# Token halves in the down projections, and linear attention's norm taken with tokens on partitions

## The reference

```python
h = layer_norm(concat([meta, x]))
h = layer_norm(alpha * h + 0.5 * swiglu(h, gate1, up1, down1))
h = layer_norm(alpha * h + token_mixer(h, w_in, ...) )
h = layer_norm(alpha * h + 0.5 * swiglu(h, gate2, up2, down2))
return h[:, N_META:]

def swiglu(h, w_gate, w_up, w_down):
    return (silu(h @ w_gate) * (h @ w_up)) @ w_down

# in token_mixer, behind one input projection: window attention (8 heads, 2 key heads, blocks of 128)
# beside gated linear attention (4 heads, both directions, chunks); its end, per head of 128 values:
    o = o * lax.rsqrt(jnp.mean(o * o, axis=-1, keepdims=True) + LN_EPS) * norm_g
    return o.reshape(b, t, GLA_WIDTH) * jax.nn.silu(g)
```

## Time and profile before

| | us |
|---|---|
| median of 3 runs | 1091.71 |
| the runs | 1092.06, 1083.59, 1091.71 |
| the profiled execution | 1082.67 |
| its span, first to last instruction | 1080.9 |
| busy: TensorE, VectorE, ScalarE | 997.0, 720.4, 382.2 |
| first down projection, from 283.5 to 396.2 | 112.7 |
| LN1 and first projections, to 428.6 | 32.4 |
| LN2, from 682.0 to 717.4 | 35.4 |
| second down projection, from 951.8 to 1059.6 | 107.8 |
| LN3 and the stores | 21.3 |

### The profile page before, as it was taken

The page is one execution under the profiler, slowest core; times in us unless marked ns, Lnnn a source line. Parts: engine busy times, 40 slices in busy tenths (PEclk is TensorE's granted clock), DMA queues, the critical chain, the costliest instruction groups (busy, mean ns, idle before and its releaser), DMA issues.

```text
span 1080.9 us, 16392 instructions
## 1 busy us (share of the span) xinstructions
PE 997.0 (92%) x6605; PEld 654.4 (61%) x6605; DVE 720.4 (67%) x1186; ACT 382.2 (35%) x488; POOL 32.3 (3%) x96
## 2 busy tenths in 40 slices
PE   3999999999899988999996889699999999989995
PEld 2888888888688875985564434434444444434443
DVE  6766666668755667767659757666666667966645
ACT  5422222224411126754334741462222223531105
POOL 0000000000000000000000000000000000000000
PEclk9999999999899998999998999889999999999998
DMA  5323232323232121111211003112323223322202
GB/s 203 107 79 109 85 110 84 109 86 110 105 108 85 68 78 32 62 64 42 77 40 40 1 1 117 40 73 83 116 78 116 96 98 127 111 78 86 104 1 79
DMA packets 23808, 88.76 MB, mean 82 GB/s; under 512 B 2907, under 2 KB 3251, under 8 KB 23763
## 3 DMA queue, kind: packets, MB, share of 16 engines
q1 hardware_dynamic: 22752, 87.17, 22.7%
q10 hardware_dynamic: 1011, 0.99, 0.3%
HBM read 86.05 MB, written 2.10 MB: 82 GB/s over the span
## 4 chain that ended last, share of the span: by engine, by line
PE 75%; DVE 16%; ACT 6%; issue 2%; DMA 0%; ACTq 0%; POOL 0%; DVEq 0%
PE PS L553 35%; PE PS L593 20%; PE PS L648 8%; DVE cmax L1413 3%; DVE wsp L1435 3%; PE PS L944 3%; ACT wsp L1059 2%; PE PS L510 2%; PE PS L632 1%; DVE big L1513 1%; ACT H L1053 1%; PE PS L770 1%; DVE X L1363 1%; PE PS L922 1%; PE PS L766 1%
## 5 line engine op out<-in xcount | busy, mean ns | idle before, releaser
L553 PE MATMUL PS<-xs,wsp 128*128 128x264 f16 (+1 forms) x3168 | 472.7, 312 | 7.5 <-ACT xs L1051 4.0
L553 PEld LDWEIGHTS PS<-xs,wsp 128*128 128x128 f16 x3168 | 311.0, 98 | 168.4 <-issue 9.6
L1059 ACT ACTIVATE wsp<-stage,wscale 128x2048 f16<-128x2048 f32 (+2 forms) x73 | 156.5, 2144 | 369.9 <-DVE wscale L1399 198.0
L1435 DVE SCALAR_TENSOR_TENSOR wsp<-stage,wscale,wsp 128x2048 f16<-128x2048 f32 (+2 forms) x73 | 184.6, 2529 | 114.3 <-ACT wsp L1059 114.3
L593 PE MATMUL PS<-big,wsp 128*128 128x264 f16 (+1 forms) x1584 | 238.6, 314 | 11.6 <-DVE big L1513 9.5
L593 PEld LDWEIGHTS PS<-big,wsp 128*128 128x128 f16 x1584 | 155.8, 99 | 94.1 <-DVE big L1513 12.8
L1413 DVE TENSOR_REDUCE cmax<-stage 128x1 f32<-128x2048 f32 (+2 forms) x73 | 179.7, 2462 | 3.9
L1447 DVE SCALAR_TENSOR_TENSOR big<-PS,oscale,tmp_a 128x528 f32 (+3 forms) x44 | 33.4, 759 | 75.7 <-ACT tmp_a L1066 75.6
L1066 ACT ACTIVATE tmp_a<-PS,oscale 128x528 f32<-128x528 f32 (+1 forms) x44 | 30.5, 694 | 136.1 <-PE PS L553 136.1
L648 PE MATMUL PS<-xs,wsp 128*128 128x264 f16 (+1 forms) x384 | 67.0, 328 | 0.1
L2007 POOL PARTITION_ALL_REDUCE call<-cmax x73 | 27.9, 382 | 979.1 <-DVE cmax L1413 979.1
(11 more groups left out here) (208 smaller groups left out, 685.1 us busy)
## 6 DMA issues: line engine op xcount, KB each, us to landing
stage<-in_gate SPq DMA_DIRECT2D x44, 512.0 KB, 3.4
stage<-in_up SPq DMA_DIRECT2D x44, 512.0 KB, 4.2
stage<-in_down SPq DMA_DIRECT2D x32, 704.0 KB, 4.9
stage<-in_w_in SPq DMA_DIRECT2D x16, 512.0 KB, 4.4
stage<-in_w_out SPq DMA_DIRECT2D x8, 512.0 KB, 4.4
X<-in_x SPq DMA_DIRECT2D x4, 512.0 KB, 6.2
out_T<-H SPq DMA_DIRECT2D x8, 256.0 KB, 2.0
stage<-in_w_in SPq DMA_DIRECT2D x2, 576.0 KB, 4.4
```

The lines of the kernel that those rows point to most:

```text
L553: return nc.tensor.matmul(dst, w, x, start=k == 0 and wp + xp == 0, stop=k == KD - 1 and xp == 1)
L1059: nc.scalar.activation(wsp[:, slot, 0, 0:cols], stage[:, slot, 0:cols], ACT.Copy, scale=wscale[:, slot:slot + 1]).then_inc(w_hi, 1)
L1435: nc.vector.scalar_tensor_tensor(wsp[:, slot, 1, 0:cols], stage[:, slot, 0:cols], wscale[:, one], wsp[:, slot, 0, 0:cols], ALU.mult, ALU.s ...
```

## The change

In both down projections tiles 0 to 4 stay whole; tiles 5, 6 and 7 are computed for the first half of the tokens, then for the second. Their weights stay in a third place (`w_extra`, in the arena), and chunks are loaded and prepared in the order 0, 1, 5, 2, 3, 6, 4, 7. The norm of half 0 runs on the other engines while TensorE multiplies half 1; half 0's mean and squares are put between the tiles of half 1. After the first down projection the first projections are taken by halves too, with other banks, and `gates(1)` comes behind both gq tiles. LN1's second half is done under them. The output leaves in 16 stores of half a tile. In LN2 VectorE takes the low half of the next chunk ahead of the last residual, the maximum behind the centring, the scale behind the reciprocals. ScalarE calls Sqrt once at the head of each norm. In the linear attention's norm the squares are the stationary operand of products with one column of `ones_dv`, so that the mean lands with tokens on partitions, 4 columns for a head; Sqrt and reciprocal run on those, the result scales an identity, and a product with `ones_dv` spreads it over the partitions into PSUM, where the last product reads it.

The diff, cut to its core:

```diff
+N_FULL = 5
+DN_ORDER = [0, 1, 5, 2, 3, 6, 4, 7]
 @@ SyncE
+                for n, q in enumerate(DN_ORDER):
+                    sp.wait_ge(w_ready, DN[f] + n - 1)
+                    load_halves(down[f][q], (DN[f] + n) % 2, DN_COLS)
 @@ TensorE, down projection
+                for q in range(N_FULL):
+                    down_tile(f, q)
+                down_tile(f, 5, 0)
+                down_tile(f, 6, 0)
+                down_tile(f, 7, 0, (KF - 3, lambda: sum_tiles(L, 0)))
+                down_tile(f, 5, 1, (8, lambda: mean(L, 0)))
+                square_sums(L, 0)
+                down_tile(f, 6, 1)
+                down_tile(f, 7, 1, (KF - 3, lambda: sum_tiles(L, 1)))
 @@ TensorE, mixer (first_proj_tiles(0) has mean(1, 1) at its third step)
+                first_proj_tiles(0)
+                square_sums(1, 1)
+                early_proj_tile(GK + 1, 0)
+                early_proj_tile(GQ, 0)
+                first_proj_tiles(1)
+                early_proj_tile(GK + 1, 1)
                 gates(0)
+                early_proj_tile(GQ, 1)
+                proj_tile(GQ + 1)
                 gates(1)
 @@ TensorE, norm
                 gla_step(1, 5)
+                norm_spread(0)
                 proj_half(AQ + 3, 1)
+                norm_spread(1)
                 proj_half(AK, 0)
                 norm_sums(2)
                 proj_half(AK, 1)
                 norm_sums(3)
                 proj_half(AV, 0)
+                norm_spread(2)
                 proj_half(AV, 1)
+                norm_spread(3)
 @@ ScalarE, mixer
+                proj_out(GQ)
                 gates_abs(0)
+                projection_hi(2)
+                proj_out(GQ + 1)
                 gates_abs(1)
-                projection_hi(2)
-                gates_ln(0)
-                proj_out(GQ)
-                proj_out(GQ + 1)
+                gates_ln(0, GV)
                 projection_hi(3)
-                proj_out(GV)
                 decays(0, 0)
                 proj_out(GV + 1)
 @@ VectorE, down projection (next_* act on the chunk that is n-th in DN_ORDER)
+                next_max(2)
+                next_scale(2)
+                next_max(3)
+                next_lo(2)
+                next_scale(3)
+                down_residual(f, 0)
+                next_lo(3)
+                next_max(4)
+                next_scale(4)
+                next_max(5)
+                next_scale(5)
+                down_residual(f, 1)
+                next_lo(4)
+                next_lo(5)
+                next_max(6)
+                next_scale(6)
+                down_residual(f, 2)
+                next_max(7)
+                next_lo(6)
+                next_scale(7)
+                next_lo(7)
+                down_residual(f, 3)
...
+                down_residual(f, 7, 0)
+                centre(L, 0)
+                down_residual(f, 5, 1)
+                half_rstd(L, 0)
+                half_norm(L, 0, 0, 4)
+                down_residual(f, 6, 1)
+                half_norm(L, 0, 4, KD)
+                down_residual(f, 7, 1)
+                centre(L, 1)
+                half_rstd(L, 1)
+                half_norm(L, 1, 0, KD)
 @@ VectorE, mixer and norm
                 projection_max(3)
+                projection_scale(3)
                 gates(0)
-                projection_scale(3)
                 gates(1)
...
+            def norm_diag(h):
+                nc.vector.reciprocal(o_root[:, h, :], o_root[:, h, :]).then_inc(o_rstd, 1)
...
+                nc.vector.tensor_tensor(o_diags[j][:, a, N_META:T].rearrange("p (b t) -> p b t", b=NB),
+                                        ident[:, :].unsqueeze(1).to_broadcast([P, NB, P]),
+                                        o_root[:, h, :].unsqueeze(2).to_broadcast([P, NB, P]), ALU.mult).then_inc(o_diag, 1)
 @@ VectorE, output projection and LN2
                 for t in range(2):
-                    residual_tile(2 * n + t, t, KD + 2 * n + t, c % 2, 2)
-
-            chunk_lo(GU[1], GU[1] % 2, GU_COLS)
-            chunk_max(GU[1] + 1, (GU[1] + 1) % 2, (GU[1] + 1) // 2, GU_COLS)
+                    if last and t:
+                        chunk_lo(c + 1, (c + 1) % 2, cols)
+                    residual_tile(2 * n + t, t, c % 2)
```

More of the change, by code:

```diff
@@ L493, in _, with sum_tiles @@
+            sp.wait_ge(out_done, 2 * 16 * KD)
         @block.tensor
         def _(pe):
-            def sum_tiles(L):
-                pe.wait_ge(x_summed, sums_before(L) + N_SUM)
-                for h in range(2):
-                    nc.tensor.matmul(PS[:, ln_bank(L, 0, h), 0:ln_width(L)], ones[:, :], x_sum[:, token_half(L, h)], start=True, stop=False)
+            def sum_tiles(L, h):
+                pe.wait_ge(x_summed, sums_before(L) + (N_SUM if L == 2 or h == 0 else KD))
+                nc.tensor.matmul(PS[:, ln_bank(L, 0, h), 0:ln_width(L)], ones[:, :], x_sum[:, token_half(L, h)], start=True, stop=False)
@@ new lines, in mean, with square_sums @@
+            def mean(L, h):
+                if L == 2:
+                    pe.wait_ge(*((res_half, 1) if h == 0 else (res_done, 2 + RES[3])))
+                else:
+                    pe.wait_ge(res_done, 2 + RES[L] + N_DN + (N_DN - N_FULL) * h)
+                nc.tensor.matmul(PS[:, ln_bank(L, 0, h), 0:ln_width(L)], ones[:, :], X[:, KD - 1, token_half(L, h)],
+                                 start=False, stop=True).then_inc(mean_ready, 1)
+            def square_sums(L, h):
+                for k in range(KD):
+                    n = ln_step(L, h, k)
+                    pe.wait_ge(squared, n + 1)
+                    nc.tensor.matmul(PS[:, ln_bank(L, 1, h), 0:ln_width(L)], ones[:, :], squares[:, n % 4, 0:ln_width(L)],
+                                     start=k == 0, stop=k == KD - 1).then_inc(sq_added, 1)
@@ L572, in gu_tile, with down_tile @@
                 mm.then_inc(gu_ready, 1)
-            def res_tile(late, r, s, w, src, kt, k_sem=None, k0=0, norm=None, split_at=None, before_b=None):
+            def down_tile(f, q, h=None, between=None):
+                i = q if h != 1 else q + N_DN - N_FULL
+                s = i % 2
+                r = RES[2 * f + 1] + i
+                pe.wait_ge(w_ready, DN[f] + DN_AT[q] + 1)
                 pe.wait_ge(res_done, r + 1)
-                for k in range(kt):
-                    if norm is not None and k == kt - 3:
-                        sum_tiles(norm)
-                    if k == split_at:
+                for k in range(KF):
+                    if between is not None and k == between[0]:
+                        between[1]()
+                    if k == KF_A:
@@ L976, in _ @@
             ffn(1)
-            layer_norm(3)
+            mean(3, 1)
+            square_sums(3, 1)
         @block.scalar
@@ new lines, in ffn @@
+                for n in range(2):
+                    down_scales(n)
+                next_max(2)
[13 more added lines that the diff above has]
+                next_max(6)
```

403 lines of the change are left out of this document (249 added, 154 removed).

## The result

The changed kernel takes 1099.56 us (median of 18 runs, 1091.10 to 1106.57) against 1089.07 for the kernel before (18 runs beside it, 1082.64 to 1092.26): ratio 1.0102, 95% interval 1.0077 to 1.0126, so 11 us slower. The forecast was 1088.5, the range ended at 1098. The profiled execution of the changed kernel took 1097.0 us, with a span of 1095.2, against 1082.67 and 1080.9.

The account below looks back on a forecast made before the run. TensorE bounds both down projections, VectorE and ScalarE handing units to each other the attention. First norm -0.1, GLA norm -0.3, second norm -5.4, second projection +4.2, clock +1.0: -0.6 on the runs' mean 1089.1 gives 1088.5 us, range 1076 to 1098.

Parts of the forecast that it names:

- The tile waits: Down projections: TensorE waits for low halves before tiles 2, 3 and 4; 4.0 us lost in first, 6.7 in second.
- The clock behind the waits: Down projections: halved clock behind tile 4's wait charged +1.0 us in the second, nothing in the first.
- Rival C: Clock falls at every hole of 2 us or more, also in down projections; +6.2 us, 1095; chance 0.18.
- The first projections: Behind the first down projection: z and gk take 5.4 us per half, 48 matmuls at 0.1125 each.
- The hole at gv tile 3: Mixer: TensorE waits 6.9 us for ScalarE's copy of gv tile 1; 2.3 us charged for halved clock behind it.
- The GLA norm: Linear attention's norm: attention starts 0.9 us later, its loop gives back 0.08 a unit; -0.3 us in all.
- The second norm: Centring starts 4.0 us earlier, TensorE keeps its clock, first tile normalised at 694.9 instead of 700.3; -5.4 us.
- The second projection and the end: Projection ends 11.6 us later, the end takes 14.4 instead of 21.9; net +4.2 us, plus 1.0 for the clock.
- The sum: Whole kernel: -0.1 - 0.3 - 5.4 + 4.2 + 1.0 = -0.6 us.
- Rival A: Down projections: the chunks keep up, so no tile waits; -12.3 us, 1077; chance 0.2.
- Rival B: Mixer: gv tiles do not wait, so the first norm gives its 9.3 us; -9.8, 1079; chance 0.12.
- Rival D: Linear attention's norm change makes the attention start earlier, -3 us more; chance 0.08, shared with something unnamed.

Follow-up runs that it names:

- gv_copy: Changed kernel with ScalarE's copy of gv tile 1 ahead of the first decays; 1.0048 against the kernel before, 5.9 us faster than the changed kernel.
- diag_first: Changed kernel with VectorE's first product with the identity ahead of the low half of chunk 8; single execution, 1092.67 us.
- lo_first: Changed kernel with the low half of chunk 4 ahead of the maximum of chunk 7 in each down projection; 1.0039 against the kernel before.
- halves_ln: Changed kernel with the old linear attention norm (sixteen reciprocals, sums over 512 columns); 1.0095 against the kernel before.
- noalt: Changed kernel with z and gk of half 0 one after the other instead of alternating every three matmuls; single execution, 1097.35 us.
- before_again: The kernel before, unchanged, profiled a second time; single execution, 1083.39 us.
- norm_only: Kernel before with only the change of linear attention's norm; 1.0024 against the kernel before, +2.6 us.
- ln2_only: Kernel before with only the second norm's order: low half ahead of the last residual, next maximum behind the centring; 0.9959, -4.5 us.
- lists: Changed kernel with VectorE's down projection operations reordered so stage slots are given back earlier; 0.9990 against the kernel before.

## Why the prediction was wrong, and where it was right

**The tile waits: right.** Predicted 0.4, 0.35 and 3.2 us in the first projection and 2.0, 0.85 and 3.9 in the second; measured 0.94, 0.60, 3.45 and 1.47, 0.99, 4.28: 5.0 against 4.0, and 6.74 against 6.75, where three misses of -0.5, +0.1 and +0.4 happen to cancel. The landing time was the weak term: 5.4 taken from the earlier trace rows, 5.6 to 6.0 in the changed kernel, gv_copy and diag_first, 7.5 in lo_first, halves_ln and noalt. Two chunks' loads now overlap (issued at 322.4 and 325.5; the DMA share from 325 to 330 is 1.02), which one chunk per tile did not; but they overlap in all six, so what makes the landing 7.5 in three of them stays open.

**The clock behind the waits: the step that failed.** The prediction charged nothing behind the 3.2 us wait and half of 2.0 behind the 3.9, on the ground that "none of the projections' or norms' holes of about 2 us has a slow stretch behind it", and that "the falls I see come 3.5 to 4.6 us into a hole". Measured 2.9 us (17.89 against 15.02) and 1.4. Behind the waits of 2.47 to 5.21 us before tile 4 of the first projection, all six profiles that have one show 1.4 to 2.9 us of loss (noalt 1.4, lo_first and halves_ln 1.7, diag_first 2.7, the changed kernel and gv_copy 2.9); behind those of 3.96 to 4.30 in the second, all five show 1.3 to 2.9. Waits of up to 1.93 us in the two down projections cost no clock in any profile. The first ground was true of one execution and taken as true of the hole: the first norm's hole of 2.23 us has a slow stretch in three executions of four (before_again). The second was a misreading of the kernel before's own trace. In the second norm TensorE is idle from 682.8 to 687.3, and its clock (busy PE, clock, DMA, GB/s) has fallen by the middle of that hole, 2.5 us into it:

```profile
683.00:685.00 2.00, 0.00 (x0) 1.00 0.00 0
685.00:687.00 2.00, 0.00 (x0) 0.58 0.66 223
```

Rival C had the mechanism, with a chance of 0.18 and 6.2 us.

**The first projections: mis-sized.** 5.4 us each for z and gk of the two halves, from 0.1125 a matmul. They took 6.9 and 7.15: +3.2 us. Cutting them in halves doubled the changes of width per column of tokens, and no term of the sum priced a change; fifteen at 0.1 us each in either half are the difference. noalt gives 1.3 back.

**The hole at gv tile 3: right.** 6.9 predicted, 6.59 measured, ended by ScalarE's copy, with a clock of 0.50 behind it (1.5 us lost, 2.3 charged). Since all that TensorE had lost before stayed lost, the first norm and mixer came to +6.3 in place of -0.1: waits +1.0, clock +2.9, width +3.2, less 0.8 for the clock behind this hole and 0.3 for its length; 0.4 is not assigned.

**The GLA norm: sign wrong, by little.** +0.9 at the attention's start predicted, +1.56 in norm_only and +3.24 in the changed kernel (1.7 of it the clock behind the 0.43 us wait); -1.2 in the loop predicted, -0.84 measured. -0.3 became +0.7, and +2.4 with the clock. The product with the identity was 0.69, not 0.85 (its lower bound was 0.7), and the eight short instructions 0.8, within their bounds. The late start of the attention is TensorE's queue order: the last spread sits behind all of AV, and VectorE waits 4.43 us for it. Whether another place would have cost less was not run.

**The second norm: right.** -5.4 predicted, -5.8 in the trace, -4.5 by runs (ln2_only). The mechanism held too: the wait for the squares went from 4.49 to 0.53 us and the clock stayed whole.

**The second projection and the end: right but 1.8 short.** +5.2 with the clock predicted, +7.0 measured: the end takes 15.0 us and not 14.4, the clock 1.4 and not 1.0, the rest lies in the half tiles. The prediction's own terms for the projection (6.7, 3.7, 0.45 and at most 0.5) add up to 11.3 or 11.4 and not to its 11.6, so by them the miss is 0.2 to 0.3 larger.

**The sum.** -0.6 + 6.4 + 2.7 - 0.4 + 1.8 = +9.9 us. The runs say +10.5 (medians) or +11 (ratio). The two profiles say +14.3, 4 more, because neither profile of the kernel before has the half clock that this one has in the attention from 616 to 626; gv_copy, with the same attention and no such stretch, has C to D 4.3 us shorter. The sizes of the clock terms are those of one execution. The range erred with the sum: its upper end was C's time and the upper group of the kernel before, never both together.

**Rival A** (the chunks keep up) was false of this list and nearly true of another, lists, with waits of 0.84, 0.51 and 1.93 us left, but at -1 us and not -12. **Rival B** (gv tiles do not wait) was false: they waited as forecast. **Rival D** (the norm lets the attention start earlier) was false: it starts 1.56 us later (norm_only).

## What to carry to other kernels

A hole in TensorE's stream costs its own length and, in some executions, half clock behind it: here 1.3 to 2.9 us behind waits of about 2.5 us and more in a projection, up to 7.6 behind one of 2.2 us in the attention. Price each new hole that way, also one of 2 us, and never conclude from one profile that a hole is free; look at the spread of the runs first. Before work is cut finer, lay out when each stage slot is given back, and give it back first: the same operations in another order were worth 12 us. Of a change with several parts, time them alone: here -4.5 us (the second norm's order) was hidden under +15, and with the list and the copies moved, the widths apart and the old norm kept, the same idea is 14 us faster than the kernel before, about 5 of it the second norm's.

## What the runs showed of the hardware

- The clock falls to half behind the attention's hole of 2.2 us in eight profiles of thirteen, with the same wait; behind the first norm's hole of 2.23 us in three of four; and behind a wait of 0.43 us in five of six. The times of the kernel before spread over 9.6 us and those of the changed kernel over 15.5, in step with the mean granted clock. What decides it stays open.
- Three matmuls with 32-column weights alternating with three of 128 cost 0.09 to 0.1 us for each change of width (0.21 us from start to start at a change, 0.11 within a group).
- GpSimd's reduction over partitions takes 0.35 us, but 3.18 when VectorE's low half runs beside it:

```profile
292.77 0.35 POOL L2209 PARTITION_ALL_REDUCE call<-cmax  x1 [18.41 <-DVE cmax L1532]
297.10 3.18 POOL L2209 PARTITION_ALL_REDUCE call<-cmax  x1 [3.98 <-DVE cmax L1532]
```

```profile
293.93 3.08 DVE L1532 TENSOR_REDUCE cmax<-stage 128x1 f32<-128x2816 f32 x1
296.93 3.14 DVE L1723 SCALAR_TENSOR_TENSOR arena<-stage,wscale,arena 128x2816 f16<-128x2816 f32 x1
```

  The reduction ends as the low half does (300.1). The Trainium skill says (SBUF — State Buffer, two separate sides) that VectorE, with two inputs in SBUF, and GpSimd exclude each other from a shared pair of ports for a whole instruction; the trace agrees. It cost 0.24 us of waiting here, since VectorE was the one at work.
